# Gather rows kept in natural order, with every eighth column as the stationary operand

## The reference

```python
def hier_moe(h, w_router_group, ..., w_gate, w_up, w_down):     # h = rmsnorm(x, norm2_w)
    ...                                    # 4 groups top-1, then 8 experts top-2: combine
    a = jnp.einsum('btd,edf->btef', h, w_gate)
    b = jnp.einsum('btd,edf->btef', h, w_up)
    act = jax.nn.silu(a) * b * combine[..., None].astype(h.dtype)
    return jnp.einsum('btef,efd->btd', act, w_down)
x = x + hier_moe(rmsnorm(x, norm2_w), ...)
```

## Time and profile before

| | |
|---|---|
| median of 3 runs | 579.58 us (579.29 to 580.82) |
| the profiled execution | 579.84 us, span 577.70 us |
| PE busy | 537.8 us (93%), 5284 matmul records |
| PEld busy | 409.9 us (71%) |
| DVE, ACT, POOL busy | 275.1, 152.6, 135.0 us |
| moved by DMA | 158.02 MB, mean 274 GB/s |
| granted TensorE clock, mean | 0.978 of full speed |

### The profile page before, as it was taken

One profiled execution on the slowest core, in us unless ns is written; L12 is line 12 of the kernel. 1 busy time (PEld: TensorE's weight loads), 2 busy tenths in 40 slices (PEclk: granted clock), 3 DMA queues, 4 the chain that ended last, 5 costly groups with the idle time before them and its releaser, 6 DMA issues. The chain is left out here.

```text
span 577.7 us, 13023 instructions
## 1 busy us (share of the span) xinstructions
PE 537.8 (93%) x5284; PEld 409.9 (71%) x5284; DVE 275.1 (48%) x803; ACT 152.6 (26%) x408; POOL 135.0 (23%) x218
## 2 busy tenths in 40 slices
PE   8999999999999999999999999999997959599974
PEld 7899999877788776879799888656454526266432
DVE  4667768782533706436856344533523231405135
ACT  3357465307841002133100124211011101010105
POOL 6687676012110090033133222000000000000001
PEclk9999999999999999999999999999997979899998
DMA  8855344749964072844378897899999999999992
GB/s 230 263 162 155 109 154 133 255 125 319 310 198 149 9 227 95 249 131 132 115 268 328 350 388 263 345 406 423 421 418 421 419 422 420 421 419 421 410 356 101
DMA packets 81229, 158.02 MB, mean 274 GB/s; under 512 B 11166, under 2 KB 65067, under 8 KB 68979
## 3 DMA queue, kind: packets, MB, share of 16 engines
q1 hardware_dynamic: 78604, 154.16, 72.9%
q10 hardware_dynamic: 2567, 3.04, 1.9%
HBM read 149.40 MB, written 7.96 MB: 272 GB/s over the span
## 5 line engine op out<-in xcount | busy, mean ns | idle before, releaser
L1416 PE MATMUL ps<-arena 128*128 128x288 f32 x480 | 122.5, 410 | 0.7 <-DVE arena L2322 0.7
L1416 PEld LDWEIGHTS ps<-arena 128*128 128x128 f32 x480 | 89.4, 190 | 26.3 <-issue 1.2
L2072 PE MATMUL ps<-arena 128*32 128x256 f32 x1024 | 63.4, 405 | 17.2 <-DMA arena<-in_w_up_dram 15.6
L1423 PE MATMUL ps<-arena 128*128 128x144 f32 x616 | 78.3, 287 | 0.0
L1423 PEld LDWEIGHTS ps<-arena 128*128 128x128 f32 x616 | 76.3, 190 | 2.5 <-issue 1.9
L2072 PEld LDWEIGHTS ps<-arena 128*32 128x32 f32 x1024 | 36.9, 117 | 42.2 <-issue 26.0
L893 POOL TENSOR_TENSOR arena<-arena 128x512 f32<-128x512 f32 x2 | 2.5, 1276 | 209.2 <-ACT arena L1329 209.2
L2347 DVE SCALAR_TENSOR_TENSOR ps<-arena,ps 128x312 f32<-128x312 f32 x72 | 39.1, 545 | 2.3 <-ACT ps L1016 0.9
L1369 PE MATMUL ps<-arena 128*128 128x128 f32 (+7 forms) x186 | 31.0, 281 | 6.3 <-DVE arena L3033 5.1
L1369 PEld LDWEIGHTS ps<-arena 128*128 128x128 f32 (+7 forms) x186 | 22.0, 147 | 15.6 <-issue 8.4
L1990 PE MATMUL ps<-arena 128*128 128x128 f32 x256 | 32.3, 279 | 0.8 <-DVE arena L3011 0.7
(11 more groups left out here) (432 smaller groups left out, 798.4 us busy)
## 6 DMA issues: line engine op xcount, KB each, us to landing
arena<-in_w_gate_dram SPq DMA_DIRECT2D x32, 1024.0 KB, 13.9
arena<-in_w_up_dram SPq DMA_DIRECT2D x32, 1024.0 KB, 16.9
arena<-in_w_down_dram SPq DMA_DIRECT2D x28, 1024.0 KB, 17.2
arena<-in_w_in_dram SPq DMA_DIRECT2D x26, 1024.0 KB, 6.5
out_dram<-arena SPq DMA_DIRECT2D x9, 512.0 KB, 7.2
arena<-in_w_branch_delta_dram SPq DMA_DIRECT2D x4, 1024.0 KB, 5.7
arena<-in_w_out_dram SPq DMA_DIRECT2D x4, 1024.0 KB, 5.2
arena<-in_state_delta_dram SPq DMA_DIRECT2D x7, 512.0 KB, 8.6
```

What stands on the lines that cost most here:

```text
L1416: last = mm(ps[n % 2][:, 0:T], w[:, k, P * (n % 2):P * (n % 2) + P], hT[:, k, :], start=(k == 0), stop=(k == KD - 1))
L1423: last = mm(to[:, 0:HT], left[:, k, :], right[:, k, :], start=(first and k == 0), stop=(k == HK - 1), skip_group_check=True)
L2072: last = mm(to[CAP * e:CAP * e + CAP, 0:FE], xgT[:, k, CAP * e:CAP * e + CAP], w[e][:, k, :], start=(k == 0), stop=(k == KD - 1))
```

## The change

POOL no longer reorders: it multiplies contiguous pieces of 256 columns and writes them where they belong, in natural order. `gathers` takes columns k, k + 8, k + 16, ... of these rows as its stationary operand, 128 of them (32 for a piece of the samples), so that the feature order of the gathered rows is as before. The step between the elements that a weight load reads goes from 4 bytes to 32 bytes. The number and the order of the instructions on each engine, their waits and their sizes stay the same.

```diff
-        x2p = b.take(2 * D).rearrange("p (n k q) -> p n k q", n=2, k=KD)
-        x2d = b.take(D // 4).rearrange("p (k q) -> p k q", k=KD)
+        x2p = b.take(2 * D).rearrange("p (n d) -> p n d", n=2)
+        x2d = b.take(D // 4)
...
                 if t == 2:
-                    nc.gpsimd.tensor_tensor(x2d, x2s.rearrange("p (q k) -> p k q", k=KD), n2bs.rearrange("p (q k) -> p k q", k=KD),
-                                            ALU.mult).then_inc(S["xp_pool"], 1)
+                    nc.gpsimd.tensor_tensor(x2d, x2s, n2bs, ALU.mult).then_inc(S["xp_pool"], 1)
                 else:
                     cols = slice(256 * j, 256 * j + 256)
-                    nc.gpsimd.tensor_tensor(x2p[:, t, :, TS * j:TS * j + TS], x2[:, t, cols].rearrange("p (q k) -> p k q", k=KD),
-                                            n2b[:, cols].rearrange("p (q k) -> p k q", k=KD), ALU.mult).then_inc(S["xp_pool"], 1)
+                    nc.gpsimd.tensor_tensor(x2p[:, t, cols], x2[:, t, cols], n2b[:, cols], ALU.mult).then_inc(S["xp_pool"], 1)
...
                 v = x2d if t == 2 else x2p[:, t]
-                v = v.rearrange("p k q -> p (k q)")
                 nc.scalar.activation(v, v, ACT.Copy, scale=rs1[:, t:t + 1]).then_inc(S["xp"], 1)
...
-                            ins = mm(to[own, :], x2d[own, k, :], G[own, 2, :],
+                            ins = mm(to[own, :], x2d[own, k::KD], G[own, 2, :],
                                      start=(first and k % 4 == 0), stop=(last_tile and k % 4 == 3), skip_group_check=True)
                     else:
-                        ins = mm(to, x2p[:, t, k, :], G[:, t, :],
+                        ins = mm(to, x2p[:, t, k::KD], G[:, t, :],
                                  start=(first and k % 4 == 0), stop=(last_tile and k % 4 == 3), skip_group_check=True)
```

More of the change, by code:

```diff
@@ L464, in hybrid_step @@
         zsum = h2T.rearrange("p k t -> p (k t)").rearrange("p (j k t) -> p j k t", j=4, k=HK)
-        dpart = x2p.rearrange("p n k q -> p (n k q)")[:, 0:2 * 6 * HT].rearrange("p (u j t) -> p u j t", u=2, j=6)
+        dpart = x2p.rearrange("p n d -> p (n d)")[:, 0:2 * 6 * HT].rearrange("p (u j t) -> p u j t", u=2, j=6)
         X_IN = {0: S["x_in"], 1: S["x_in1"], 2: S["x_in2"]}
```

## The result

The changed kernel takes **593.52 us** (592.75 to 594.63, 4 runs) against 580.18 us of the kernel before on the same chip (579.29 to 580.82, 4 runs): a ratio of 1.0235 with a 95% interval of 1.0222 to 1.0248, 13.3 us slower. The profiled execution took 593.85 us with a span of 591.8 us.

A forecast was written before the change was run, and what follows sets the result against it. DMA loading of expert weights was taken to bound the kernel from 375 us on. Delays of 4.1 us at quad 0, 6.9 at downs 2 and 7.2 at ups 7 summed to 18.2 us, giving 597.8 us; range 579 to 602.

The forecast's parts named there:

- POOL's part: POOL's products before quad 0's gather: contiguous and shorter, but hidden since ACT waits for DVE; worth nothing.
- Is the load the pace setter: Gather on PE: weight loads, at about 117 ns per 128 columns, set its pace, so nothing covers a slower load.
- The price of a strided load: Gather's weight loads: 215 ns for 128 columns, 54 for 32; 1.57 us more per tile, 1.79 for the samples.
- the high price: Strided weight loads cost DVE's strided time per element, 1.68 ns per column; chosen over 0.9 ns and a middle price.
- Y: Added time of one quad's gather, two tiles plus the samples: 4.93 us.
- Step 1: Quad 0's gather delays its gate products and SP's next loads in full: 4.1 us.
- Step 2: Downs 2 loads, behind the gathers for quads 1 and 2: 9.9 us later against a 3.0 cushion, a 6.9 us hole.
- Step 3: Quads 3 to 5: PE falls 17.8 us behind, about 19 us of load waits and lower clock absorb it; hidden.
- Step 4: Ups 7 loads, behind the gathers for quads 6 and 7: 9.9 us later against a 2.7 cushion, a 7.2 us hole.
- 0.1 ns per column more: Dearer-load rival, 5%: each such increment adds 0.3 us to two tiles, 0.5 to Y, 2.5 to the time.
- Costs nothing: Rival for the gather's strided loads: no slowdown, time stays at 579.6 us; 27% chance.

The follow-up runs named there:

- four pieces of 32 columns: Changed kernel with each tile's strided stationary operand taken as four loads of 32 columns, same output: 582.51 us, ratio 1.0046; repeated with more rounds, 583.62 us.
- kernel with quad 0 alone: Changed kernel, but only quad 0's gather takes every eighth column, the others neighbouring ones: 583.18 us, ratio 1.0067.
- kernel for quads 6 and 7: Changed kernel, but only the gathers for quads 6 and 7 take every eighth column, the others neighbouring ones: 586.71 us, ratio 1.0101.
- one with eight steps: Changed kernel with tile loads stepping 1 in quad 0 up to 8 in quad 7, samples contiguous; 16 loads took 1.98 us at step 2, 3.81 at 4.

## Why the prediction was right, and where it was off

The path was right: the gather sets the time where it delays SP's loads beyond a cushion, and nowhere else. The measured 13.3 us are less than the 18.2 of the sum, though, and the range from 579 to 602 held "nothing changes" too, so that lying in it says little. Two things were wrong behind the number, how the samples' loads add up and why a strided load is slow, and the errors of the two prices had opposite signs. By its steps:

- **POOL's part, zero.** Shown by the kernel with the new layout alone, 1.0004. Its product took 0.73 us and not 0.65.
- **Is the load the pace setter.** Right: 16 loads went from 1.87 to 3.88 us and the matmuls with them.
- **The price of a strided load.** For a tile 215 ns was taken, 241 were measured, so that a tile costs +2.0 us and not 1.57: the high price, DVE's time per element, was still low. Its reason does not hold: it was taken "since the step costs at the side of the memory", and the four pieces of 32 columns read the same elements from the same partitions at 0.9 ns each. That 1.88 ns per column came out near DVE's 1.68 is luck as far as the runs show. For the samples +1.79 us was taken and 0.06 measured. This is the term that was mis-sized most: 64 loads at 54 ns each were added up, as if the loads of the four pieces came one after the other. One such load does take longer (135 ns against 105), but the pieces overlap. Y was thus 2 x 2.01 + 0.06 = 4.1 us in place of 4.93.
- **Step 1 of the sum.** 4.1 predicted, 3.7 in the trace: 1.26 us too much for the samples, 0.9 too little for the tiles. The kernel with quad 0 alone has 3.7 as well.
- **Step 2.** A hole of 6.9 predicted, 5.2 measured. SP's loads of downs 2 came 46.7 us after those of gates 2 (373.52 to 420.18) and 38.5 before; the 8.2 us between these, less the cushion of 3.0, are 5.2.
- **Step 3.** Quads 3 to 5 hidden: shown, 0.9995 alone. In the changed kernel PE's waits for ups loads fell from 15.6 us to 1.5.
- **Step 4.** 7.2 predicted, about 4.4 by the remainder (13.3 - 3.7 - 5.2). The measured Y explains 1.7 of the difference (9.9 - 8.2). The rest is in a rule that step 3 had used and step 4 left out: PE's last wait for ups before quad 6 was followed by products at a lower clock, and with a shorter wait they were not. The up products of quad 5, before and after:

```profile
503.84 5.67 PE L2072 MATMUL ps<-arena 128*32 128x256 f32 x64 [5.84 <-DMA arena<-in_w_up_dram]
```

```profile
513.64 3.66 PE L2069 MATMUL ps<-arena 128*32 128x256 f32 x64 [1.23 <-DMA arena<-in_w_up_dram]
```

The granted clock of these stretches is 0.63 in the first and 1.00 in the second. A shorter wait alone does not do it: quad 3's up products took 5.35 us at 0.68 in the changed kernel too, with no wait for a load ahead of them. PE so comes 2.0 us earlier to quad 6, measured from the landing of the weights, and gives 0.8 back later, when the samples' gather for quad 7 took 2.73 us in place of 1.95:

```profile
545.08 2.73 PE L1984 MATMUL ps<-arena 32*32 32x128 f32 x64
```

8.2 - 2.7 - 2.0 + 0.8 gives 4.3.

- **A slip in the rivals.** 0.1 ns per column more adds 16 x 128 x 0.1 ns, 0.2 us, to each tile, so 0.4 and not 0.3 us to the two, 0.6 to Y and 3.0 to the time; 1.9 ns would be 604 and not 603.
- **The rivals.** "Costs nothing" was wrong for the tiles, though true for the samples. The rule in the Trainium skill (TensorE: Matmul & The Clock Gate, "LDWEIGHTS (loading the stationary operand)"), that a load's time depends on the number of columns alone, holds for steps of 1 and 2 here (1.87 and 1.98 us) and not from 3 on. The Trainium skill's note on cachelines (SBUF — State Buffer, under "Door 1: The DMA port swizzle"), that two accesses to a 16-byte line are needed for full speed, agrees with the rows: steps 1 and 2 are at or near full speed, 3 to 8 are not. The Trainium skill's figure of 4 f32 as a free step, in the same note, does not agree with 3.81 us.

## What to carry to other kernels

For f32, read the stationary operand with a step of at most two elements. Or take it in four pieces of 32 columns, which hid the step in the loads here but left the kernel 0.3 to 0.6% slower than before. Let an engine off the path do the reordering, since its strided time can be free.

Where a queue of loads bounds a stage, added work on another engine costs nothing, all of it, or all but a cushion. For each group of loads take the first landing less the landing on an idle queue: this is the cushion. Add up how much later what releases the group comes, counted since the engine last waited for a load. Only what passes the cushion counts.

## What was not expected of the hardware

- Four strided loads on different columns of the array overlap although they read the same partitions: 64 loads of 32 columns at a pace of 27 ns, though one takes 140, against 241 ns for one load of 128 columns with the same step.
- A step of 3 f32 adds half of what one of 4 or more adds: 2.90 us for 16 loads against 1.87 at step 1 and 3.81 at step 4.
- With a shorter wait ahead of them quad 5's up products kept the full clock: the 64 records after a wait of 5.84 us took 5.67 us at a granted clock of 0.63, those after 1.23 us took 3.66 at 1.00.
- Right behind a tile's strided loads the samples' gather for quad 7 got the lower clock and took 2.73 us (2.80 in the kernel for quads 6 and 7, 2.85 in the one with eight steps, where the samples' loads are contiguous), against 1.95 before. The same sequence for quads 1 to 6 took 1.98 us; what sets them apart is not shown.
